# Four norms done in two token halves inside the neighbouring matmul stages, and the third tile's weight split moved into the first tile's processing

## What is computed

```python
lat = lat + 0.5 * mod[:, 0, 2] * _swiglu(_modulate(lat, norm_g[i, 0], mod[:, 0, 0], mod[:, 0, 1]), ffn_w13[i, 0], ffn_w2[i, 0])
cx = cx + 0.5 * modc[0, 2] * _swiglu(_modulate(cx, ...), ffn_w13[i, 0], ffn_w2[i, 0])
h = _modulate(lat, norm_g[i, 1], mod[:, 1, 0], mod[:, 1, 1])
...
lat = lat + mod[:, 1, 2] * y
```

## Time and profile before

| | us |
|---|---|
| median of 3 runs | 2079.53 (2076.51 to 2079.58) |
| the profiled execution | 2075.76 |
| its span | 2073.9 |
| PE busy | 1906.5, mean granted clock 0.965 of full speed |
| DVE busy | 1397.0 |
| ACT busy | 689.9 |
| POOL busy | 128.0 |

### The profile page before, as it was taken

The page is one execution under the profiler, slowest core; times in us unless marked ns, Lnnn a source line. Parts: engine busy times, 40 slices in busy tenths (PEclk is TensorE's granted clock), DMA queues, the critical chain, the costliest instruction groups (busy, mean ns, idle before and its releaser), DMA issues.

```text
span 2073.9 us, 26722 instructions
## 1 busy us (share of the span) xinstructions
PE 1906.5 (92%) x10092; PEld 1621.9 (78%) x10092; DVE 1397.0 (67%) x2081; ACT 689.9 (33%) x926; POOL 128.0 (6%) x78
## 2 busy tenths in 40 slices
PE   2986799799999998998999999999999998879998
PEld 2955788688888877876888888778888887669998
DVE  7878899876666666668666666676665226755554
ACT  2454355422222223332222222232222213444432
POOL 2001200200000110003000001100000010010000
PEclk9987899799999999998999999999999999999999
DMA  9843854423443452334333444433343233223444
GB/s 378 319 169 78 227 199 176 174 105 138 152 152 133 157 187 112 136 138 171 118 131 146 152 144 155 178 114 132 148 152 108 96 110 113 83 82 142 168 160 158
DMA packets 75738, 315.79 MB, mean 152 GB/s; under 512 B 19060, under 2 KB 22904, under 8 KB 56344
## 3 DMA queue, kind: packets, MB, share of 16 engines
q1 hardware_dynamic: 75136, 314.15, 42.7%
q10 hardware_dynamic: 536, 0.79, 0.1%
HBM read 313.86 MB, written 1.06 MB: 152 GB/s over the span
## 4 chain that ended last, share of the span: by engine, by line
PE 74%; DVE 18%; ACT 3%; issue 2%; DMA 1%; POOL 1%; SPq 0%; DVEq 0%; ACTq 0%
PE acc L1318 72%; DVE Wl L832 4%; ACT Wh L527 2%; DVE tmp L819 2%; PE psN L1318 1%; DVE psGT L861 1%; DVE psGT L867 1%; DVE psGT L864 1%; DVE najunk L867 1%; DVE najunk L864 1%; DVE small L989 1%; DVE XT L819 1%; DMA afirst<-in_ada_w 1%; PE psN L1380 1%; DVE tmp L1007 1%
## 5 line engine op out<-in xcount | busy, mean ns | idle before, releaser
L1318 PE MATMUL acc<-Hh,Wh 128*128 128x512 f32 (+1 forms) x2320 | 808.4, 348 | 48.7 <-DVE Hl L819 23.3
L1318 PE MATMUL acc<-Hl,Wh 128*128 128x512 f32 (+1 forms) x2320 | 799.5, 345 | 0.0
L1318 PE MATMUL acc<-Hh,Wl 128*128 128x512 f32 (+1 forms) x2320 | 798.9, 344 | 0.0
L832 DVE TENSOR_TENSOR Wl<-raw,Wh 128x2048 fp32r<-128x2048 f32 (+1 forms) x214 | 449.6, 2101 | 270.3 <-ACT Wh L527 270.2
L1318 PEld LDWEIGHTS acc<-Hh,Wh 128*128 128x128 f32 x2320 | 447.9, 193 | 112.9 <-issue 46.7
L527 ACT ACTIVATE Wh<-raw 128x2048 fp32r<-128x2048 f32 (+1 forms) x214 | 374.3, 1749 | 343.0 <-PE acc L1318 329.6
L1318 PEld LDWEIGHTS acc<-Hl,Wh 128*128 128x128 f32 x2320 | 448.5, 193 | 50.4 <-issue 0.7
L1318 PEld LDWEIGHTS acc<-Hh,Wl 128*128 128x128 f32 x2320 | 447.4, 193 | 50.5
L1318 PE MATMUL acc<-hidh,Wh 128*128 128x512 f32 (+1 forms) x704 | 258.6, 367 | 0.9 <-DVE Wl L832 0.9
L1318 PE MATMUL acc<-hidl,Wh 128*128 128x512 f32 (+1 forms) x704 | 258.3, 367 | 0.0
L1318 PE MATMUL acc<-hidh,Wl 128*128 128x512 f32 (+1 forms) x704 | 258.2, 367 | 0.0
(11 more groups left out here) (222 smaller groups left out, 1187.7 us busy)
## 6 DMA issues: line engine op xcount, KB each, us to landing
raw<-in_ffn_up SPq DMA_DIRECT2D x88, 1024.0 KB, 4.8
graw<-in_mod_w SPq DMA_DIRECT2D x144, 512.0 KB, 5.5
raw<-in_ffn_down SPq DMA_DIRECT2D x64, 704.0 KB, 4.1
graw<-in_ada_w SPq DMA_DIRECT2D x32, 512.0 KB, 5.7
raw<-in_odd_in SPq DMA_DIRECT2D x16, 1024.0 KB, 4.9
raw<-in_even_in SPq DMA_DIRECT2D x12, 1024.0 KB, 7.0
raw<-in_conv_in SPq DMA_DIRECT2D x12, 1024.0 KB, 4.8
afirst<-in_ada_w SPq DMA_DIRECT2D x8, 1024.0 KB, 13.0
```

The costliest lines, as they stand in the source:

```text
L832: nc.vector.tensor_tensor(Wl[:, half, 0:f], raw[:, slot, 0:f], Wh[:, half, 0:f].bitcast(f32), ALU.subtract)\
L1318: return nc.tensor.matmul(out, lhsT, rhs, start=start, stop=stop)
```

## The change

1. **Four norms by halves** (`HALVED`: conv_in, ffn1_up, ffn2_up, gqa_kv). The stage before ends with its last output block (its last tile in conv_out) done for the latent columns first and for the context columns after, in two PSUM banks. `lat_done` is counted after the latent part. While PE does the context part, the latent tokens' residual, square, sums (in psN), means, power and spread are made; the context's sums go to the bank psT[1]. Then DVE and ACT make the eight chunks of the latent half, with the context's residual, square and means between them, and then the eight chunks of the context half.
2. **The first two tiles of the next stage** are done in the order tile 0 latent, tile 1 latent, tile 0 context, tile 1 context (`first_two_halved`; for gqa_kv the keys' latent half, the value tile's latent tokens, the keys' context half, the value tile's context tokens). Both tiles' weights are split in halves of 1024 columns between the chunks; behind conv_out the first tile's stays whole. `tile_done` for both comes only behind the context parts.
3. **Third tile.** In ffn1_up and ffn2_up (`PAIRED`) the third tile's split is moved from the head of step 1 into step 0, behind the tanh on ACT and behind the second product on DVE.
4. **Modulations**: conv_out makes one row per tile instead of two, gqa_out one instead of none.

The diff, cut to its core; bodies are moved left by two levels, and on ACT and DVE `norm` begins with the branch for the halves:

```diff
-    ("conv_out", 4, 16, 0, TOK, 2, "dve"),
+    ("conv_out", 4, 16, 0, TOK, 1, "dve"),
...
-    ("gqa_out", 4, 16, 0, LAT, 0, "dve"),
+    ("gqa_out", 4, 16, 0, LAT, 1, "dve"),
...
+if name in ("ffn0_down", "ffn1_down", "ffn2_down"):
+    drained[by] -= 1
...
+HALVED = {n: i for i, n in enumerate(["conv_in", "ffn1_up", "ffn2_up", "gqa_kv"])}
+LAST = {n: (KC - 2, KC - 1) if n == "ffn1_up" else (KC - 1,) for n in HALVED}
...
+        if name in HALVED:
+            pool.wait_ge(lat_mean, HALVED[name] + 1)
+            power(rstd[:, 0:2], means[:, 0:2], 2).then_inc(lat_rstd, 1)
+            pool.wait_ge(n_mean, i + 1)
+            power(rstd[:, 2:4], means[:, 2:4], 2).then_inc(n_rstd, 1)
+            return
         pool.wait_ge(n_mean, i + 1)
...
+    def split_half(n, j):
...
+        nc.scalar.activation(Wh[:, n % SPLIT, c], raw[:, n % RAW, c], ACT.Copy).then_inc((hi_half, hi_ready)[j], 1)
...
     def splits(s):
         name = summed_of(s)
         for t in range(s.tiles):
+            if halved(s) and t == s.tiles - 1:
+                if s.tiles < KC:
+                    act.wait_ge(drained["dve"], s.drained0 + t)
+                    square(name, 2 * t - 2)
+                    square(name, 2 * t - 1)
+                    next_split(s, t, t % PER, t // PER)
+                    act.wait_ge(lat_res, HALVED[name] + 1)
+                else:
+                    act.wait_ge(lat_res, HALVED[name] + 1)
+                for k in LAST[name]:
+                    if k == LAST[name][0]:
+                        act.wait_ge(n_sum, SUM0[name] + 5)
+                    square_half(name, k, CL)
+                return
...
     def norm(name, squares=None):
         i, n = NORMS[name], NORM_TOK[name]
+        if name in HALVED:
+            n0, ffn = S[name].n0, S[X_FROM[name]].tiles > KC
+            if ffn:
+                split_half(n0, 0)
+            for k in range(KC):
+                if k == 1 and ffn:
+                    split_half(n0, 1)
+                if k in (4, 6):
+                    split_half(n0 + 1, k // 2 - 2)
+                act.wait_ge(lat_t, KC * HALVED[name] + k + 1)
+                nc.scalar.activation(Hh[:, k, CL], tmp[:, k % 2, CL], ACT.Identity, bias=affine(name, k, 0)[1])\
+                    .then_inc(lat_hi, 1)
+                if k == 2:
+                    act.wait_ge(drained["dve"], S[X_FROM[name]].drained1)
+                    for q in LAST[name]:
+                        square_half(name, q, CC)
+            for k in range(KC):
+                act.wait_ge(n_t, KC * i + k + 1)
+                nc.scalar.activation(Hh[:, k, CC], tmp[:, k % 2, CC], ACT.Identity, bias=affine(name, k, 1)[1])\
+                    .then_inc(n_hi, 1)
+            return
...
         def step(t, u, i):
-            next_split(s, t, u, i)
+            if not (s.name in PAIRED and isinstance(t, int) and t < 2):
+                next_split(s, t, u, i)
             act.wait_ge(tile_done, s.n0 + t + 1)
...
+            if s.name in PAIRED and isinstance(t, int) and t == 0:
+                split(s.n0 + 2)
...
+    def halves_norm(name, meanwhile):
...
+        dve.wait_ge(lat_done, l + 1)
+        residual_half(0, CL).then_inc(lat_res, 1)
+        meanwhile()
+        mean(0, psN, lat_ss, l + 1).then_inc(lat_mean, 1)
+        if not ffn:
+            split(S[name].n0)
+        dve.wait_ge(lat_spread, l + 1)
+        scaled(0, 0, CL, psN).then_inc(lat_t, 1)
+        for k in range(KC):
+            if k + 1 < KC:
+                if k > 0:
+                    dve.wait_ge(lat_ready, KC * l + k)
+                scaled(k + 1, 0, CL, psN).then_inc(lat_t, 1)
+            if ffn and k < 2:
+                split_half(S[name].n0, k)
+            dve.wait_ge(lat_hi, KC * l + k + 1)
+            low(k, 0, CL).then_inc(lat_ready, 1)
+            if k in (5, 7):
+                split_half(S[name].n0 + 1, k // 2 - 2)
+            if k == 2:
+                dve.wait_ge(tile_done, s.n0 + s.tiles)
+                residual_half(1, CC).then_inc(drained["dve"], 1)
+            if k == 5:
+                mean(1, psT[1], n_ss, i + 1).then_inc(n_mean, 1)
+        dve.wait_ge(n_spread, i + 1)
+        scaled(0, 1, CC, psT[1]).then_inc(n_t, 1)
+        for k in range(KC):
+            if k + 1 < KC:
+                if k > 0:
+                    dve.wait_ge(h_ready, H0[name] + k)
+                scaled(k + 1, 1, CC, psT[1]).then_inc(n_t, 1)
+            dve.wait_ge(n_hi, KC * i + k + 1)
+            low(k, 1, CC).then_inc(h_ready, 1)
...
         def step(t, u, i):
+            if halved(s) and isinstance(t, int) and t == s.tiles - 1:
+                modulation_of(s, t, u, i)
+                return
...
+    def first_two_halved(s):
+        name, prev = s.name, S[X_FROM[s.name]]
+        l = HALVED[name]
+
+        def part(t, c, ready, base, beside):
+            n = s.n0 + t
+            for k in range(KC):
+                pe.wait_ge(ready, base + k + 1)
+                for j in range(2):
+                    last = three(acc[t][j][:, c], n % SPLIT, j * KC + k, Hh[:, k, c], Hl[:, k, c], k == 0, k == KC - 1)
+                if k in beside:
+                    beside[k](name)
+            return last
+
+        pe.wait_ge(lo_ready, s.n0 + 1)
+        part(0, CL, lat_ready, KC * l, {3: ctx_sums, 7: ctx_spread})
+        pe.wait_ge(lo_ready, s.n0 + 2)
+        pe.wait_ge(drained["dve"], prev.drained1)
+        part(1, CL, lat_ready, KC * l, {})
+        part(0, CC, h_ready, H0[name], {}).then_inc(tile_done, 1)
+        part(1, CC, h_ready, H0[name], {}).then_inc(tile_done, 1)
...
+    def lat_sums(name):
+        pe.wait_ge(lat_sq, LAT_SQ0[name] + len(LAST[name]))
+        for q in LAST[name]:
+            for b in range(2):
+                ins = nc.tensor.matmul(psN[:, b:b + 1], tmp[:, q % 2, b * P:(b + 1) * P], ones[:, 0:1],
+                                       start=False, stop=q == KC - 1, skip_group_check=True)
+        ins.then_inc(lat_ss, 1)
...
+    def ctx_sums(name):
...
+            if halved(s) and isinstance(t, int) and t == s.tiles - 1:
+                for h, hc in enumerate((CL, CC)):
+                    for j in range(2):
+                        for k in range(KC):
+                            last = three(acc[u % 2][h][:, j * LAT:(j + 1) * LAT], u % 2, j * KC + k, xh[:, k, hc], xl[:, k, hc],
+                                         k == 0, k == KC - 1)
+                        if h == 0 and j == 1:
+                            sum_of_sums(X_TO[s.name])
+                        if h == 1 and j == 0:
+                            lat_sums(X_TO[s.name])
+                    last.then_inc((lat_done, tile_done)[h], 1)
+                lat_spreads(X_TO[s.name])
+                return
...
-        if begin:
+        if begin or halved(s):
...
+        elif s.name in HALVED:
+            first_two_halved(s)
...
+        def last_halved():
+            name, t = X_TO[s.name], s.tiles - 2
+            pe.wait_ge(drained["dve"], s.drained0 + t - 2)
+
+            def part(h, w, cols, beside=None):
+                pe.wait_ge(lo_ready, s.n0 + t + w + 1)
+                for k in range(W2H):
+                    kk = w * W2H + k
+                    last = three(acc[1][h][:, cols], w, k, hidh[:, kk, cols], hidl[:, kk, cols], kk == 0, kk == FC - 1)
+                    if beside and k == 4:
+                        beside(name)
+                return last
+
+            part(0, 0, CL)
+            sum_of_sums(name)
+            part(0, 1, CL).then_inc(lat_done, 1)
+            part(1, 0, CC, lat_sums).then_inc(tile_done, 1)
+            lat_spreads(name)
+            part(1, 1, CC).then_inc(tile_done, 1)
...
+        if name in HALVED:
+            for h, bank in enumerate((psN, psT[1])):
+                for b in range(2):
+                    nc.tensor.matmul(bank[:, b:b + 1], tmp[:, 2, (2 * h + b) * P:(2 * h + b + 1) * P], ones[:, 0:1],
+                                     start=b == 0, stop=False, skip_group_check=True)
...
-    for k in range(KC):
-        pe.wait_ge(h_ready, H0["gqa_kv"] + k + 1)
-        for j in range(2):
-            last = three(acc[0][j][:, :], n0 % SPLIT, j * KC + k, Hh[:, k, :], Hl[:, k, :], k == 0, k == KC - 1)
-    last.then_inc(tile_done, 1)
+    keys(CL, lat_ready, KC * HALVED["gqa_kv"])
...
+    pe.wait_ge(drained["dve"], S["ffn2_down"].drained1)
     vh, vl = (w[:, (n0 + 1) % SPLIT, :].rearrange("p (j k n) -> p j k n", j=2, k=KC) for w in (Wh, Wl))
     for tb in range(4):
+        if tb == 2:
+            keys(CC, h_ready, H0["gqa_kv"]).then_inc(tile_done, 1)
...
-        if tb == 1:
+        if tb == 2:
...
```

More of the change, by code:

```diff
@@ L212, in build @@
         c_tanh = sem("c_tanh")
+        hi_half = sem("hi_half")
+        lat_done, lat_res, lat_sq, lat_ss, lat_mean, lat_rstd, lat_spread, lat_t, lat_hi, lat_ready = (
+            sem("lat_" + x) for x in ("done", "res", "sq", "ss", "mean", "rstd", "spread", "t", "hi", "ready"))
         nmx = small[:, 0:64]
@@ L292, in build, with halved @@
```

(43 more changed lines are left out.)

41 lines of the change are left out of this document (36 added, 5 removed).

## The result

The kernel after takes 2063.62 us (median of 4 runs, 2062.47 to 2063.9), the kernel before 2078.02 beside it (2076.19 to 2079.58): ratio 0.993, 95% interval 0.9913 to 0.9947. It is faster by 14.4 us, 2068.6 were forecast. The profiled execution took 2063.7 with a span of 2061.9, against 2075.76 and 2073.9 before; the profile before was 2.3 us under the median of its kernel, the one after lies on it. So of the 14.4 us the two traces can explain 12.0.

What follows compares the result with a forecast made beforehand. TensorE, busy 92% of the span, bounds the kernel, so time lies only where it waits. Gains 3.1 + 4.7 + 3.1 + 3.6 less 3.6 make 10.9 us, taking the median from 2079.53 to 2068.6, range 2061.5 to 2078.5.

Steps and rivals of the forecast that it cites:

- Half-width matmuls: First two tiles after each halved norm: 256-column matmuls take 0.12 us each, making 23.0 us of PE instead of 21.8.
- The rival of more gain by free halves: Two half-width matmuls cost no more than a whole, 6 us back, gqa_out 2.4: about 2062 us, chance 0.12.
- The order behind ffn_down: Norm behind ffn_down: chain up to latent spread hidden, second tile's weights at 28.4 us, second tile ends at 45.7.
- The third tile's weights: Third tile after the norm: split and low part end at 45 to 45.7 us, hidden with nothing to spare.
- ffn1_up: Norm behind conv_out: from its last tile's start to the second tile's end 45.2 us instead of 49.9, gain 4.7.
- With one per tile that goes: conv_out: one modulation per tile removes DVE's late start of the last residual, 967.77 though PE's tile was whole by 964.5.
- The moved modulations: Four modulations leave conv_out for gqa_out, whose last residual then starts 3.6 us later (bounds 2.4 and 5).
- the slower rival: Clock stays low through both latent parts in each norm, 6.1 us lost each: 2093 us, chance 0.07.
- the mild one: Clock low for 3 to 6 us per norm, +1.5 to 3 each, total 2075 to 2079 us, chance 0.13.
- the forecast's own sign: Tile 0's latent part: clock 1.00 would show the forecast right, a clock under 1 would show it wrong.
- The term of 0.213 us for a matmul at the lower clock: Latent chunks at low clock: six matmuls of 0.213 us make a chunk 1.28 us instead of 0.91.
- the evidence that the clock stays up: gqa's attention, PE 32.1 busy of 41 us at clock 1.00, cited for the clock staying at 2.4 GHz.

Runs made afterwards that it cites:

- e2_third_late: Kernel after with the third tile's weight split back at the head of step 1 in ffn1_up and ffn2_up; 2066.14 us, ratio to before 0.9945.
- e6_mods_in_ffn2_down: Kernel after with the ten modulations of gqa_kv, gqa_q and gqa_out made in ffn2_down's first ten steps; 2058.39 us, ratio to before 0.9908.
- e1_mods_back: Kernel after with modulations where they were, two per tile in conv_out and none in gqa_out; 2066.01 us, ratio to before 0.9943.
- e4_no_second_low: Kernel after without nearly all of the second tile's low part of the weights in the four norms; 2056.54 us, ratio to before 0.9906.
- e5_mods_alone: Kernel before with only the four modulations moved, norms whole and third split as before; 2074.35 us, ratio to before 0.999.

## Why the prediction was right, step by step

**Direction and range were right; the time was forecast 5.0 us too high.** 1.5 of them are the median of before (2079.53 from three runs, 2078.02 from the four beside the kernel after). 1.1 are the sum, 10.9 where the traces differ by 12.0. The other 2.4 are that the traced execution of before lies 2.3 under its kernel's median and that of the kernel after on it. That 10.9 comes so near to 12.0 is luck: every part of the sum came out a little better than forecast, 14.6 together, and 1.9 were lost again to the clock in places that the sum left out.

**Half-width matmuls: right.** The second tile's context half is whole 5.76 after the first's (799.55 to 805.31) at clock 1.00, 0.12 each. The isolated-matmul rule of "TensorE: Matmul & The Clock Gate" of the Trainium skill (Back-to-back issue gap), 109 ns by my estimate, would have made these 48 some 0.5 us shorter. Here each has a weight load, and the rows decide for 0.12. The rival of more gain by free halves falls.

**The order behind ffn_down: right, its terms a little too dear.** DVE's chunks began 0.3 sooner. Its half splits took 1.22 as estimated, but the next operation starts 1.14 behind each (775.29 to 776.43), 4.6 for the 4.9; residual and mean took 0.5 for 0.64; the waits for ACT came to 1.0 for 1.3 (0.50, 0.35 and 0.18 at 781.15, 782.50 and 786.06). That is 1.1 at the second tile's weights and some 0.8 at its end, at each of the three norms behind an ffn_down. The power of two columns is 0.71, not 1.02; hidden, it made no difference.

**The third tile's weights: right.** Hidden by 1.0 us, and by 0.55 at conv_in (804.76 for 805.31); e2_third_late prices the new place at 2.5 us in all.

**ffn1_up: the size nearly right, its cause only half.** I forecast 4.7 for both parts, 5.4 came. The two-by-two of runs says whose: the move alone brings 4.7, the halves on top of it 0.7, the halves without it -1.3 (about 51.2, taking the third tile whole at 950.0, 144.3 after conv_in's second as in the other kernels, to 1001.23). "With one per tile that goes" was the step that carried the stage. The halves bring little here. My reading, which no run tests, is that conv_out's last tile is 11 us and not 15 long, so that the early sums come too soon: PE waits 0.59 for POOL's adds (955.86). One term was missed on the way:

```profile
960.84 2.28 DVE L902 TENSOR_TENSOR Wl<-raw,Wh 128x2048 fp32r<-128x2048 f32 x1
961.00 2.69 POOL L467 TENSOR_TENSOR rstd<-means,expo 128x2 f32<-128x2 f32 x1 [5.19 <-DVE means L978]
...
963.74 0.43 PE L1611 MATMUL psN<-ident,rstd 128*128 128x128 f32 x2
```

(kernel after.) The power started beside a whole weight split and took 2.69 instead of 0.71. PE was in the context half until then, so it stayed hidden, to the last tenth. Another is the clock, below.

**The moved modulations: right, 3.4 for 3.6.** I had one dot of 2.32 per tile; there were two, of 1.77 and 1.59, 0.9 over 1.23 together, and a tile took 6.6. POOL's two adds took 3.95 beside a split and two dots and 3.42 beside the split alone. The rule of the Trainium skill, "SBUF — State Buffer" (Who interferes with whom), that a DVE operation with two SBUF inputs and GpSimd's reads exclude each other, fits.

**The clock.** At three norms it stayed at 1.00 in tile 0's latent part (774.20 to 788.00, 1333.40 to 1347.20, 1703.70 to 1720.00), and the slower rival falls. At ffn1_up the mild one came true, by the forecast's own sign (a clock under 1 there):

```profile
970.00:976.00 6.00, 5.71 (x34) 5.42 (x35) 5.41 (x11) 3.12 (x6) 0.70 (x1) 0.72 0.00 0
```

PE was busy 2.71 of the 5 us before, with one hole of 1.5. The price is small: PE ends the latent part 0.4 us after the second tile's weights are there (976.48 for 976.09). In e6_mods_in_ffn2_down, where the fall came sooner (0.66 over 965 to 970), the same stretch is 44.0 and not 44.5. The term of 0.213 us for a matmul at the lower clock agrees with the 0.21 of e1_mods_back.

The greater loss is around gqa's attention, which I had cited as the evidence that the clock stays up. From the last q tile to gqa_out's first residual PE has the same 220 matmuls in every kernel traced here, and the time follows the clock:

| kernel | us | mean clock |
|---|---|---|
| before | 57.25 | 1.00 |
| e4_no_second_low | 57.3 | 1.00 |
| e6_mods_in_ffn2_down | 58.6 | 0.97 |
| after | 60.0 | 0.94 |
| e1_mods_back | 61.8 | 0.92 |

The other four lie between, at 58.2 to 60.1 and clocks of 0.97 to 0.94. What PE did in the 8 us before does not tell the kernels apart: in the kernel after it is busy 6.12 before the drop to 0.79; in e6_mods_in_ffn2_down, at the same time of the span, 5.23, and the clock of the next 8 us is 1.00, to fall at the end of the attention:

```profile
1766.00:1774.00 8.00, 5.23 (x24) 2.96 (x23) 5.30 (x13) 2.79 (x6) 1.01 (x1) 1.00 0.31 121
1774.00:1782.00 8.00, 6.78 (x31) 4.25 (x32) 5.48 (x17) 4.37 (x12) 0.00 (x0) 1.00 0.00 0
...
1814.00:1822.00 8.00, 6.66 (x33) 5.77 (x34) 3.02 (x6) 2.55 (x3) 0.00 (x0) 0.79 0.00 0
```

What brings it on stays open; no run was made on it. It is up to 4.5 us from one trace to another, more than the 3.4 between the shortest and the longest of four executions of the kernel before, and so the smaller differences here are read from stretches and not from medians.

## What to carry to other kernels

Where a serial chain (a norm) stands between two long stages of matmuls, cut the tokens in two and let the chain of one half run beside the other half's matmuls; how much it hides differed with what stands ahead of the chain (3.9 us behind a block of 15 us, 0.7 behind one of 11; that the length is the reason was not tested). Look at what else stands in the chain's queue before you cut: here four dot pairs in the wrong stage (conv_out) cost 4.7 us at ffn1_up, more than the 3.9 that the halves of a norm bring behind an ffn_down, and put into gqa_out they gave 3.4 of it away again. Moving all fourteen into the one stage with room gave 4.7 us more by the stretches (7.4 by the medians, the rest being mostly the clock) with the same work. And don't take another stage's stretch as the floor for this one: compare with a version in which the lateness is gone.

## What the hardware showed that was not expected

- POOL's power has a price by columns, 0.71 us for two and 1.02 for four, and 2.69 for two when DVE's whole weight split runs beside it (961.00).
- A DVE add of two columns took 1.05 us instead of 0.16, at 954.77 in the kernel after, where POOL's adds ran (952.03, 3.77 for two).
- Sums of 128x1 cost by the clock too: sixteen took 3.57 us at clock 0.50, behind 3.85 us of idle PE (kernel before), and 1.95 at 0.97, behind 1.6 (e5_mods_alone).
- The clock falls in gqa's attention in the traces of seven kernels and not in those of two (before and e4_no_second_low, 57.3 us), with the same 220 matmuls of PE there, at a price of 0.9 to 4.5 us. Each trace is one execution.
